# The tail of a mixture-of-experts kernel: last expert rows loaded and normalised per token tile, part of the sums on GpSimd

## The reference

```
idx = top_k(...)                       # 6 of 64 experts per token
wts = scores[idx] / sum * 2.5
routed = sum over the 6 of  swiglu(h, w_gate[e], w_up[e], w_down[e]) * w
x = x + g2 * (routed + shared)
return rms_norm(x, final_g)            # x * rsqrt(mean(x*x) + eps) * final_g
```

## Time and profile before

| | us |
|---|---|
| median of 3 runs | 2594.6 (2591.66 to 2595.86) |
| profiled execution, its own time | 2594.43 |
| its span (first to last instruction) | 2592.7 |
| TensorE busy | 2466.0 (95%) |
| VectorE busy | 1031.2 (40%) |
| ScalarE busy | 658.8 (25%) |
| GpSimd busy | 582.3 (22%) |

### The profile page before, as it was taken

How to read it: one execution, slowest core, us unless ns; L and a number is a source line. 1 busy time by engine, 2 the same in 40 slices (tenths; PEclk the granted TensorE clock), 3 DMA queues, 4 the chain that set the end, 5 groups by cost and what they waited for, 6 DMA issues and landing times. The chain is left out here.

```text
span 2592.7 us, 33982 instructions
## 1 busy us (share of the span) xinstructions
PE 2466.0 (95%) x12385; PEld 1462.4 (56%) x12385; DVE 1031.2 (40%) x2342; ACT 658.8 (25%) x1323; POOL 582.3 (22%) x558
## 2 busy tenths in 40 slices
PE   8999999999999999999999999999999999999994
PEld 7546888544666558886454544555555434444441
DVE  1126888302323256663013333666542323322226
ACT  2214444301333221221013553233122111111111
POOL 3017888300000024540103100111111111111110
PEclk9999999999999999999999999999989999999997
DMA  4225555542211233232323212101054899999997
GB/s 141 77 78 166 165 162 162 139 97 71 58 49 49 65 89 90 81 94 70 89 55 96 68 35 53 29 27 35 26 195 181 353 422 413 402 390 396 397 390 289
DMA packets 292226, 404.76 MB, mean 156 GB/s; under 512 B 14434, under 2 KB 253752, under 8 KB 267520
## 3 DMA queue, kind: packets, MB, share of 16 engines
q1 hardware_dynamic: 275136, 366.18, 41.1%
q0 software_dynamic: 15632, 34.44, 4.1%
q10 hardware_dynamic: 1328, 2.38, 0.2%
HBM read 396.20 MB, written 27.71 MB: 164 GB/s over the span
## 5 line engine op out<-in xcount | busy, mean ns | idle before, releaser
L957 PE MATMUL bank<-bring 128*128 128x512 f32 x704 | 303.2, 592 | 0.0
L1704 PE MATMUL bank<-bring 128*64 128x512 f32 (+1 forms) x512 | 235.2, 614 | 17.3 <-issue 16.5
L957 PEld LDWEIGHTS bank<-bring 128*128 128x128 f32 x704 | 133.5, 190 | 166.1 <-issue 165.7
L1018 PE MATMUL bank<-ysq 128*128 128x256 f32 x960 | 213.7, 379 | 0.0
L1018 PEld LDWEIGHTS bank<-ysq 128*128 128x128 f32 x960 | 182.4, 190 | 24.8
L2260 DVE TENSOR_TENSOR xT<-bank,xT 128x512 f32<-128x512 f32 x32 | 22.1, 691 | 362.3 <-PE bank L957 362.2
L1018 PE MATMUL bank<-hT,bring 128*128 128x256 f32 x640 | 146.5, 382 | 3.0 <-issue 3.0
L721 POOL TENSOR_TENSOR ysq<-ysq 128x512 f32<-128x512 f32 x23 | 29.3, 1272 | 501.4 <-ACT ysq L1800 443.8
L1704 PEld LDWEIGHTS bank<-bring 128*64 128x64 f32 (+1 forms) x512 | 79.9, 161 | 103.7 <-issue 103.6
L730 POOL TENSOR_TENSOR two<-two 128x1024 f32<-128x1024 f32 (+2 forms) x72 | 122.0, 1694 | 58.2 <-ACT two L1820 36.9
L1018 PEld LDWEIGHTS bank<-hT,bring 128*128 128x128 f32 x640 | 122.6, 192 | 20.7 <-issue 3.9
(11 more groups left out here) (528 smaller groups left out, 4235.8 us busy)
## 6 DMA issues: line engine op xcount, KB each, us to landing
bring<-f_w_in SPq DMA_DIRECT2D x88, 512.0 KB, 5.2
bring<-exp_w_gate SPq DMA_DIRECT2D x32, 1024.0 KB
bring<-exp_w_up SPq DMA_DIRECT2D x32, 1024.0 KB
bring<-exp_w_down SPq DMA_DIRECT2D x32, 1024.0 KB
two<-ada_w SPq DMA_DIRECT2D x24, 1024.0 KB, 5.3
bring<-f_w_down SPq DMA_DIRECT2D x16, 1408.0 KB, 7.1
two<-exp_w_gate SPq DMA_DIRECT2D x16, 1024.0 KB
two<-exp_w_up SPq DMA_DIRECT2D x16, 1024.0 KB
```

What stands on the lines that cost most here:

```text
L957: mm = pe.matmul(ps[BANKS[stage][n % 4]][:], w[:, k, n % per * P:(n % per + 1) * P], rhs[:, k, :], start=(k == 0), stop=(k == kb - 1))
L1018: mm = pe.matmul(ps[bank][:, 256 * half:256 * half + 256], weights[:, k, :], rhs[:, k, :], start=(k == 0), stop=(k == 3))
L1704: mm = pe.matmul(ps[3][m * h:m * h + m, :].rearrange("p (m n) -> p m n", m=2), hgT[par][:, k, m * h:m * h + m], w, start=(k == 0), stop=(k ...
```

## The change

Four things are different.

1. The load of j = 5 is issued as four transfers of one token tile each (512 KB) in place of two of two tiles each. The tiles count up four semaphores (`LAST_Y`): those of `Y_SEMS[5]` for tiles 0 and 1, and those of `Y_SEMS[0]`, one step further, for tiles 2 and 3.
2. VectorE runs `combine(4)` for tiles 0 and 1 only (`LATE = 2`). For tiles 2 and 3, GpSimd does the same sum in two instructions per tile: a `tensor_scalar` that multiplies `yrows(4, t)` by its weight in place, and a `tensor_tensor` that adds it to `yrows(0, t)`. It begins a tile when that tile's sum over j = 0 to 3 is there. It counts up `pool_order`.
3. VectorE's `combine(5)` and the norms are interleaved: sum of tile 0, sum of tile 1, norm of tile 0, sum of tile 2, norm of tile 1, sum of tile 3, norms of tiles 2 and 3. The sums of tiles 2 and 3 wait for GpSimd.
4. The counts that ScalarE waits for are two lower, since GpSimd's sums do not count up `y_summed`.

```diff
@@ names
+        LAST_Y = [(Y_SEMS[5][0], y_loaded(5, 0)), (Y_SEMS[5][1], y_loaded(5, 1)),
+                  (Y_SEMS[0][0], y_loaded(0, 0) + 16), (Y_SEMS[0][1], y_loaded(0, 1) + 16)]
+        LATE = 2
@@ SyncE
             sp.wait_ge(s("y1_stored"), 16 * (last // 2 + 1))
-            results_in(5, 0, Y_SEMS[5][0])
-            results_in(5, 1, Y_SEMS[5][1])
+            for t in range(TT):
+                rows = y_dram.rearrange("(t p j) d -> p t j d", p=P, j=8)[:, t, 5, :]
+                sp.dma_start(yrows(5, t), rows).then_inc(s(LAST_Y[t][0]), 16)
@@ GpSimd, after its last scatter
+            for t in range(LATE, TT):
+                pool.wait_ge(s(Y_SEMS[4][1]), y_loaded(4, 1))
+                pool.wait_ge(s("y_summed"), 3 * TT + t + 1)
+                nc.gpsimd.tensor_scalar(yrows(4, t), yrows(4, t), wj[:, t, 4:5], None, ALU.mult).then_inc(s("pool_order"), 1)
+                pool.wait_ge(s("pool_order"), 2 + 2 * (t - LATE) + 1)
+                nc.gpsimd.tensor_tensor(yrows(0, t), yrows(4, t), yrows(0, t), ALU.add).then_inc(s("pool_order"), 1)
@@ ScalarE
-                act_e.wait_ge(s("y_summed"), 5 * TT + t + 1)
+                act_e.wait_ge(s("y_summed"), 4 * TT + LATE + t + 1)
@@ VectorE
-            def combine(j):
-                for t in range(TT):
+            def combine(j, ts=range(TT)):
+                for t in ts:
...
-            for j in range(2, 5):
+            for j in range(2, 4):
                 combine(j)
+            combine(4, range(LATE))
...
             overflow_rounds(dve, overflow_expert, beyond, end=combined_again)
-            combine(5)
...
-            for t in range(TT - 1):
-                last_norm(t)
+            for t in range(TT):
+                dve.wait_ge(s(LAST_Y[t][0]), LAST_Y[t][1])
+                if t < LATE:
+                    dve.wait_ge(s("y_summed"), 4 * TT + t + 1)
+                else:
+                    dve.wait_ge(s("pool_order"), 2 + 2 * (t - LATE) + 2)
+                weighted(5, t).then_inc(s("y_summed"), 1)
+                if t:
+                    last_norm(t - 1)
             last_norm(TT - 1)
```

More of the change, by code:

```diff
@@ L2919, in beyond @@
                 if r == 0:
+                    dve.wait_ge(s("pool_order"), 2 + 2 * (TT - LATE))
                     for par in range(2):
```

## The result

The changed kernel takes 2601.12 us in the median of 13 runs (2597.27 to 2604.66), against 2594.6 us (2590.92 to 2597.77, 13 runs) for the kernel before: a ratio of 1.0025 with a 95% interval of 1.0016 to 1.0033. It is 6.5 us slower. Forecast were 2597.4 us and a range up to 2600.2; the time lies 0.9 us above the range. A loss was forecast, but less than half of the measured one.

The account below looks back on a forecast made before the run. TensorE is busy nearly everywhere, but VectorE's sums and norms bound the last 8.05 us; turns with GpSimd add 2.9 us to 2594.43, giving 2597.3, plus about 0.2 for the median, stated as 2597.4 us; range 2594.2 to 2600.2.

Parts of the forecast that it names:

- The price of the `tensor_scalar`: GpSimd's multiply for j = 4, tiles 2 and 3: 1.1 us each, taken between bounds of 0.95 and 2.35.
- The rival with the dear `tensor_scalar`: GpSimd's multiply takes 2.35 us, each of two turns grows by 1.25: +5.4 us, 2599.8 us; chance 0.12.
- GpSimd's start: GpSimd may begin j = 4, tile 2 at about 2572.5, when the j = 3 sum of that tile is done.
- From there GpSimd is done and its two results are in time: After VectorE's j = 5, tile 1 sum (2584.33): GpSimd's adds, the second ending at 2583.25, delay neither sum 2 nor 3.
- The last store follows as before: After the last norm, forecast to end at 2592.52: the closing store took 3.1 us to the span's end before.
- The turns: In j = 4 and 5, VectorE and GpSimd alternate by whole instructions; after the other's end a sum needs 1.08 us.
- the rival without turns: VectorE and GpSimd run side by side in the tail: -0.9 to +0.4 us, middle 2594.2 us; chance 0.10.
- A late first use: GpSimd's first `tensor_scalar` is slow to begin; a 4 to 5 us delay gives 2598.3 to 2599.3 us; chance 0.08.
- The interleaving: Norms between the j = 5 sums: waiting for ScalarE replaces waiting for the load, -0.9 to +0.4 us without GpSimd's cost.
- the table load losing its cover: At norm 0: ScalarE's root comes 2.80 us behind sum 0, table load included, while sum 1 fills only 1.20.

Follow-up runs that it names:

- The run with one tile: The changed kernel with only tile 3 of j = 4 on GpSimd (`LATE = 3`); ratio 1.0002 to the kernel before.
- the run with GpSimd's half only: The changed kernel with the two loads of two tiles and all sums ahead of all norms put back; ratio 1.0015 to the kernel before.

## Why the prediction was wrong

*The price of the `tensor_scalar`* is the step that failed first. I bounded it by 0.95 and 2.35 us and took 1.1, from a select of 128 columns. It is 2.86 us alone, outside the bounds: nothing excluded that a one-input operation is longer than the add. That is 3.5 us more of GpSimd's time in two instructions. The rival with the dear `tensor_scalar` named this cause, at 2.35 us, and gave 2599.8 us. With 2.86 us its sum would give +2.9 + 3.5 = 6.4 us, all but the 6.5 measured, but only by luck: VectorE's last norm ended 4.3 us later in the tail, not 6.4, and the drain, which is in no sum of the prediction, brought the rest.

*GpSimd's start* failed second. The working began at 2572.5, when the j = 3 sum was there. In the diff a second wait stood ahead of it, for the j = 4 load, and the trace of before said of it only that it landed before 2576.26. It landed 2.05 us behind the issue of the j = 5 load after, which would be 2575.6 on the clock of before: 3 us later than assumed, all of it in front of GpSimd's chain. No run moved this start alone.

*"From there GpSimd is done and its two results are in time"* failed for these two reasons together. I had the second add end at 2583.25, 9.7 us behind the load's issue; it ended at +15.9, 6.2 us later, where the price (3.5) and the start (3.1) make 6.6. Sum 3 waited 2.30 us.

*"The last store follows as before"* failed for a third reason, which no row that I had chosen showed and which I did not look for: GpSimd's drain of 9.2 us, harmless at 2583.8, became the last thing in the program. It costs 1.95 us here.

*The turns* were right for operations with two inputs, and the rival without turns falls. After an end on GpSimd a VectorE instruction of 1024 columns needs 1.08 us (2584.60 to 2585.68), as worked out, and GpSimd's add ends 2.21 us behind VectorE's end (2582.39 to 2584.60, 2589.12 to 2591.33), against 2.22. The `tensor_scalar` does not take its turn as a whole, as I had it: it holds VectorE off for only some 1.1 of its 2.86 us. In the changed kernel its last 2.86 us, counted back from its end, begin at 2578.27, and the sum that started at 2579.15 took 1.32 us, 0.04 more than alone. The second begins at 2585.53 by the same count, and the sum at 2585.60 took 2.13, as if let in at 2586.65, 1.12 us in. The run with one tile gives 1.11 us by the same count. That near 1.1 is also what I had taken for the whole instruction is luck, and it hid the wrong price from VectorE's turns, but not from GpSimd's end. The Trainium skill (SBUF — State Buffer, Who interferes with whom) says that a VectorE instruction with two SBUF inputs contends with a GpSimd instruction that reads SBUF. The trace agrees, except that this one blocks for less than half of its length.

*A late first use* did not come: with VectorE at rest, the first `tensor_scalar` of its execution started 0.1 us behind its load and took 2.86 us, in the run with GpSimd's half only.

*The interleaving* was booked at -0.9 to +0.4 us by itself. Without GpSimd's work it is +1.5 in one tail (and not to be seen in the time), since VectorE does not reach the first sum earlier while it keeps all of j = 4. The part of it that I named, the table load losing its cover, was right: 1.63 us of wait, 0.35 with the table loaded early. In the changed kernel it is 0.90.

The sum as it should have been, on the tail: first sum 1.5 earlier; waits and turns on VectorE 5.8 later; drain 1.95 later; together 6.2, against 2.9 forecast.

What stays open: why a waiting `tensor_scalar` missed changes of VectorE's instructions that an add did not miss (5.92 and 5.09 us), and what the drain waits for. In the four kernels with no late work on GpSimd it takes 9.21 us from its entry.

## What to carry to other kernels

Work moved to an idle engine is paid for three times if it comes late: in what its consumer waits, with everything queued behind that consumer; in the turns that it takes from VectorE; and in what its engine still has to do when the program ends. Before moving it, list every wait of the first instruction with the time at which it is met, loads first, and read the closing rows of each engine's queue. An operation that the trace does not show has no upper bound from its neighbours: measure it alone.

## What the hardware showed that was not expected

- GpSimd's closing drain ends 9.2 to 9.3 us behind the engine's last work, in the eight runs that had such work late, from a 0.1 us memset to a chain of four; SyncE's takes 0.01 us.
- On GpSimd, float32, 128x1024: `tensor_scalar` 2.86 us (2.77 with an immediate), `tensor_tensor` add 2.34, `tensor_tensor` with the second input broadcast from one column 1.89.
- A `tensor_scalar` on GpSimd that met an unbroken row of VectorE instructions took 5.92 and 5.09 us, where it takes 2.86 with VectorE at rest.
